# Splitting each weight unit of the second block's attention inputs with two operations of 1024 columns in place of four of 512

## The reference, cut to what matters

```
def second_block(x, g_mix, w_in, q_norm_a, ...):
    h = rms_norm(x, g_mix)
    proj = h @ w_in
    a_qkv = proj[..., :A_QKV].reshape(Bsz, S, 3, A_HEADS, HEAD_DIM_2)
    b_qkv = proj[..., A_QKV:A_QKV + B_QKV].reshape(Bsz, S, 3, B_HEADS, HEAD_DIM_2)
...
    qa = head_rms(a_qkv[:, :, 0], q_norm_a).transpose(0, 2, 1, 3)
```

## Time and profile before

| what | value |
|---|---|
| median of 3 runs | 2525.06 us |
| the profiled execution's own time | 2522.77 us |
| its span on the core | 2521.0 us |
| busy PE, DVE, ACT, POOL | 2501.6, 1684.4, 1226.2, 276.3 us |
| splits of this stage | 240 on ACT (L1491), 240 on DVE (L1863), from 1082.7 to 1450 us |

### The profile page before, as it was taken

How to read it: one execution, slowest core, us unless ns; L and a number is a source line. 1 busy time by engine, 2 the same in 40 slices (tenths; PEclk the granted TensorE clock), 3 DMA queues, 4 the chain that set the end, 5 groups by cost and what they waited for, 6 DMA issues and landing times.

```text
span 2521.0 us, 38233 instructions
## 1 busy us (share of the span) xinstructions
PE 2501.6 (99%) x13066; PEld 2134.5 (85%) x13066; DVE 1684.4 (67%) x2663; ACT 1226.2 (49%) x2144; POOL 276.3 (11%) x297
## 2 busy tenths in 40 slices
PE   9999999999999999999999999999999999999999
PEld 7888888888888888878888888888888888888888
DVE  7787889958885788576555554457575565665664
ACT  6656655434443444456566554445453443443442
POOL 0000215303330233040000000001100000000000
PEclk9999999999999999999999999999999999999999
DMA  7454545665555556646555456655465556555554
GB/s 245 159 169 162 168 134 191 194 211 183 188 193 194 186 187 192 206 125 205 183 179 177 155 175 194 196 187 198 153 216 192 192 184 200 187 197 189 187 194 134
DMA packets 197232, 463.75 MB, mean 184 GB/s; under 512 B 17482, under 2 KB 45166, under 8 KB 197102
## 3 DMA queue, kind: packets, MB, share of 16 engines
q1 hardware_dynamic: 196430, 459.91, 56.0%
q0 software_dynamic: 672, 2.11, 0.3%
HBM read 459.81 MB, written 2.14 MB: 183 GB/s over the span
## 4 chain that ended last, share of the span: by engine, by line
PE 83%; DVE 9%; issue 3%; ACT 3%; DMA 1%; DVEq 0%; SPq 0%; POOL 0%; ACTq 0%; POOLq 0%
PE G L845 46%; PE SB L845 34%; DVE wlo L1874 3%; PE MB L845 2%; DVE wlo L1863 1%; ACT y L1619 1%; ACT whi L1504 1%; DVE y L2130 1%; DMA raw<-in_in 1%; PE SB L1424 0%; DVE hS L1932 0%; DVE x L1924 0%; DMA x<-in_xT 0%; PE SB L1345 0%; DVE og L2213 0%
## 5 line engine op out<-in xcount | busy, mean ns | idle before, releaser
L1874 DVE TENSOR_TENSOR wlo<-raw,whi 128x1024 fp32r<-128x1024 f32 x446 | 546.3, 1265 | 81.6 <-ACT whi L1504 70.8
L845 PE MATMUL SB<-whi,hS 128*128 128x512 f32 x1728 | 546.8, 393 | 0.0
L845 PE MATMUL G<-hS,whi 128*128 128x512 f32 (+1 forms) x2240 | 534.5, 391 | 2.4 <-DVE hS L2331 1.2
L1871 DVE TENSOR_TENSOR wlo<-raw,whi 128x1024 fp32r<-128x1024 f32 (+1 forms) x304 | 352.1, 1199 | 262.1 <-ACT whi L1501 261.1
L1504 ACT ACTIVATE whi<-raw 128x1024 fp32r<-128x1024 f32 x446 | 449.0, 1051 | 127.9 <-PE SB L845 63.3
L845 PEld LDWEIGHTS G<-hS,whi 128*128 128x128 f32 x2240 | 409.6, 188 | 86.9 <-issue 3.4
L1501 ACT ACTIVATE whi<-raw 128x1024 fp32r<-128x1024 f32 (+1 forms) x304 | 298.7, 1029 | 352.7 <-PE SB L845 289.2
L845 PEld LDWEIGHTS SB<-whi,hS 128*128 128x128 f32 x1728 | 325.4, 188 | 67.2
L845 PE MATMUL SB<-wlo,hS 128*128 128x512 f32 x864 | 337.1, 390 | 0.0
L1605 ACT ACTIVATE tmp<-G 128x256 f32<-128x256 f32 x231 | 87.8, 380 | 503.9 <-PE G L845 503.9
L845 PE MATMUL G<-aS,whi 128*128 128x512 f32 x1248 | 300.3, 391 | 0.0
(11 more groups left out here) (237 smaller groups left out, 2281.4 us busy)
## 6 DMA issues: line engine op xcount, KB each, us to landing
raw<-in_up SPq DMA_DIRECT2D x304, 512.0 KB, 4.5
raw<-in_dn SPq DMA_DIRECT2D x216, 512.0 KB, 4.4
raw<-in_in SPq DMA_DIRECT2D x192, 256.0 KB, 3.6
raw<-in_in SPq DMA_DIRECT2D x64, 512.0 KB, 4.7
raw<-in_out SPq DMA_DIRECT2D x64, 512.0 KB, 4.4
raw<-in_mix SPq DMA_DIRECT2D x64, 512.0 KB, 4.0
raw<-in_mix SPq DMA_DIRECT2D x32, 384.0 KB, 3.7
raw<-in_in SPq DMA_DIRECT2D x32, 192.0 KB, 3.0
```

The lines of the kernel that those rows point to most:

```text
L845: return pe.matmul(o, w, m, start=start, stop=stop, skip_group_check=half_first)
L1871: dve.tensor_tensor(group_weights(wlo, slot, half, depth(st, k)), group_raw(h0 % RAW_SLOTS, depth(st, k)), group_weights(whi, slot, half, ...
L1874: dve.tensor_tensor(wlo[:, slot, a * P:b * P], raw[:, h0 % RAW_SLOTS, 0:(b - a) * P], whi[:, slot, a * P:b * P].bitcast(F32), ALU.subtract ...
```

## The change

A unit is split by two operations on ACT and two on DVE. Each covers two pieces, 1024 columns: two neighbouring slots of `raw8` are read with the row tile outside and the slot inside (8 runs of 128 columns), and 4 runs of 256 columns are written. ACT waits for both slots to have landed; each operation raises `hi_done` or `lo_done` by two. The loads, their waits and the order of everything else on every queue stay.

```diff
@@ -340,6 +340,10 @@
+        def in2_raw(at):
+
+            return raw8[:, at:at + 2, :].rearrange("p c (k n) -> p k c n", k=KPG)
+
@@ -1484,12 +1488,13 @@
                 if st.name == "in2":
                     dst = whi[:, slot, :].rearrange("p (k c n) -> p k c n", k=KPG, c=PARTS)
-                    for part in halves:
+                    for part in (0, 2):
                         j = st.piece(it, k, part) - st.pbase
-
-                        act.wait_ge(landed8[IN2_SLOT(j)], LANDED8[j])
-                        act.activation(dst[:, :, part, :], raw8[:, IN2_SLOT(j), :].rearrange("p (k n) -> p k n", k=KPG),
-                                       ACT.Copy).then_inc(hi_done, 1)
+                        at = IN2_SLOT(j)
+
+                        act.wait_ge(landed8[at], LANDED8[j])
+                        act.wait_ge(landed8[at + 1], LANDED8[j + 1])
+                        act.activation(dst[:, :, part:part + 2, :], in2_raw(at), ACT.Copy).then_inc(hi_done, 2)
                     return
@@ -1857,11 +1862,11 @@
                     h_w, l_w = (w[:, slot, :].rearrange("p (k c n) -> p k c n", k=KPG, c=PARTS) for w in (whi, wlo))
-                    for part in halves:
+                    for part in (0, 2):
                         j = st.piece(it, k, part) - st.pbase
-                        dve.wait_ge(hi_done, st.piece(it, k, part) + 1)
-                        dve.tensor_tensor(l_w[:, :, part, :], raw8[:, IN2_SLOT(j), :].rearrange("p (k n) -> p k n", k=KPG),
-                                          h_w[:, :, part, :].bitcast(F32), ALU.subtract).then_inc(lo_done, 1)
+                        dve.wait_ge(hi_done, st.piece(it, k, part) + 2)
+                        dve.tensor_tensor(l_w[:, :, part:part + 2, :], in2_raw(IN2_SLOT(j)),
+                                          h_w[:, :, part:part + 2, :].bitcast(F32), ALU.subtract).then_inc(lo_done, 2)
                     return
```

## The result

The changed kernel takes 2528.35 us (median of 20 runs, 2526.97 to 2530.97); the kernel before took 2523.43 us on the same chip (20 runs, 2522.41 to 2525.88). The ratio is 1.0019, with a 95% interval of 1.0013 to 1.0025: 4.9 us or 0.19% slower. The forecast was 2527.2 us: 4.4 us over the profiled execution of before (2522.77), and 3.8 us over this median of 20 runs.

A forecast was written before the change was run, and what follows sets the result against it. The prediction took PE, busy 2501.6 of 2521.0 us, as the bound. To the profiled execution's 2522.77 it added 1.54 us at the first turning and 2.9 for the clock: 2527.2 us, range 2522.5 to 2530.0.

The forecast's parts named there:

- Cost of an operation: Split of a unit on DVE: 2.36 us in two operations against 2.48 in four, 0.12 us gained.
- Turns of POOL and DVE: Units 4 to 6: folds and subtractions alternate strictly; a subtraction's turn takes 1.08 us for 1024 columns, 0.55 before.
- A later start: In the seam DVE waits for ACT's longer first copy; unit 4's copy starts 0.45 us later, bounds 0 and 1.2.
- Unit 4: Before group 1: two turns in place of four, PE starts 1.03 us earlier, its 2.73 us wait shrinking to 1 or 1.5.
- The row sums: After group 1's start: POOL's folds end at 1133.00, PE waits 3.34 us, and the sums come 2.36 us later.
- The clock: Behind the new wait at the row sums: 5.8 us at half clock, costing +2.9 us.
- The first turning: Attention's first turning: at 1147.32 without a wait, +1.54 us without the clock, ACT at about the old time.
- The seam's own wait: Before the second half's turning: PE's wait grows by about the later start or more, costing little at the end.
- The steady part: Units after the first turning, 350 us: three tight turnings lose 0.06 us each, 0.2 us in all.
- the clock holds: Rival: the clock stays full behind the new wait at the row sums, total 2524.4 us; chance 0.13.
- POOL is not held up: Rival at the folds: DVE lacks unit 6 or POOL gets two turns for one; 2523.1 to 2525 us, chance 0.23.
- slower: Rival: the steady part's slack is used up, turnings lose some 6 us; above 2530.1, about 2533 us; chance 0.10.

The follow-up runs named there:

- e5: Pairs on both engines in units 4 to 6 only, fours elsewhere, against the kernel before: 2525.65 us, ratio 1.0010.
- e3: Pairs on both engines in units 7 to 59 only, fours in units 0 to 6, against the kernel before: 2525.13 us, ratio 1.0007.
- e4: Pairs on both engines in units 0 to 3 only, fours elsewhere, against the kernel before: 2524.06 us, ratio 1.0001.
- e7: The changed kernel with POOL's ten folds working on one column each, run once: 2523.88 us, against 2528.25 us for the change's profiled execution.
- e8: Fours everywhere, ACT's copies of unit 4 before its eight squarings, PE's row sums four row tiles later, against the kernel before: 2521.00 us, ratio 0.9990.
- e1: ACT copies in pairs as in the change, DVE subtracts in fours as before, against the kernel before: 2526.94 us, ratio 1.0012.
- e2: DVE subtracts in pairs as in the change, ACT copies in fours as before, against the kernel before: 2528.64 us, ratio 1.0019.
- e6: The whole change with PE's row sums four row tiles later (`NORM6 = 12`, not 10), against the kernel before: 2527.55 us, ratio 1.0020.
- e9: Units 7 on divided 512, 512, 1024 on both engines, the others in fours, against the kernel before: 2524.23 us, ratio 1.0004.

## Why the prediction was right, step by step

PE's lag behind the kernel before (start of the same matmul, the lag at 1080 us taken off), at four times of the trace of before:

| kernel | 1126.5 | 1144.5 | 1158 | 1515 |
|---|---|---|---|---|
| after | -0.4 | 4.8 | 3.8 | 5.0 |
| e5 (units 4 to 6) | -1.4 | 3.9 | 2.9 | 2.9 |
| e3 (from unit 7) | 0.0 | 0.0 | 1.0 | 2.2 |
| e4 (units 0 to 3) | 0.9 | 1.0 | 1.2 | 1.2 |
| e7 (tiny folds) | -0.2 | -0.2 | -0.2 | 1.0 |
| e8 (unit 4 early, fours) | -3.8 | -3.3 | -1.7 | -1.8 |

- **Cost of an operation: right.** 2.36 us for a unit, as in the earlier trace rows; and the 120 operations less on each engine gave nothing, since PE is the bound.
- **Turns of POOL and DVE: right.** One fold, one subtraction, in strict turn, to the end of the folds. e1 (fours on DVE) and e7 (folds of one column) take the wait away, each from its side.
- **A later start: size off.** "I take 0.45 us in all for the start of unit 4's copy." It was 1121.03 - 0.48 - 1119.59 = 0.96, inside the bounds of 0 and 1.2. The two subtractions of unit 0 run back to back, and POOL's second scaling, which now starts together with them, gets no turn: 3.68 us, where it took 2.07 before and 1.58 is what it takes undisturbed. In e1 and e2, with pairs on one engine only, it takes 2.55 and 2.60 us, and PE's wait at the first half's turning is 0.2 and 0.3 us: the 1.4 us need pairs on both. PE's turning of the first half comes 1.4 us late, and DVE's addition waits for PE. So the first subtraction started 1.45 us later, not 1.04.
- **Unit 4: half right.** The wait of 2.73 us shrank to nothing, not to 1 or 1.5, because PE itself came 2.3 us late out of the seam. Where the seam was left as it was (e5) the wait was 1.3 us.
- **The row sums: place and size right.** The wait was 3.44 us (forecast 3.34). The sums were 3.2 us late, not 2.36; the rest is the later start.
- **The clock: mis-sized.** "I take the same 5.8 us at half clock behind it: +2.9." It was 3.4 us, a loss of 1.7; the wait's length, from which I took the figure, does not set that of the half clock (last section).
- **The first turning: right, for a reason that was half wrong.** PE came without a wait. But the scalings were not ready "at about the old time": they ended at 1147.85, 1.6 us later than before with the lag taken off, and only PE's own lateness covered it. To this point the balance was +3.8 us; the prediction's terms give 1.54 + 2.9 = 4.4. The later start made it more, the clock less.
- **The seam's own wait: right in effect, larger in size.** It grew from 3.4 to 4.6 + 1.4 us, yet units 0 to 3 in pairs cost only 0.6 us (e4; its interval holds zero).
- **The steady part: mis-sized.** "0.2 in all", and it was 1.2 us (e3: 1.2; e7: 1.2). I had looked at the turnings alone, and missed the output step at 1185 us, where two late splits add up.

There is luck in the total. The forecast was added to one execution (2522.77), near the median of 20 runs (2523.43); added to the median of three, 2525.06, it would have come to 2529.5. And +4.9 us against +4.4 is near because two terms that were too small (start, steady part) and one that was too large (clock) partly cancel. The mechanism and its order hold without that luck: e5 shows half of the loss with units 4 to 6 alone, e3 a third with units 7 to 59. The rival "the clock holds" was wrong by one window (0.66); "POOL is not held up" by the ten folds of 16.19 us; "slower", the used-up slack, was the right idea for the steady part at a fifth of its price.

What stays open: what decides whether half clock comes and lasts 3.4 or 6.8 us, how much of each profile's sum this is, and whether the 0.6 us of e4 are real.

## What to carry to other kernels

In this kernel merging two operations of an engine that is not the bound gained nothing. Count what gets coarser: the engine behind it starts after the whole merged operation (here a unit is done 0.35 us later, though both engines are busy for less), and an engine that takes turns with it is held off for longer (here 1.08 us in a turn in place of 0.55). When a wait is removed by moving its reader or one unit of work, look for every other reader of the same late data, on all engines, before counting the gain: of 3.7 us won by the start of group 1 in e8, 1.8 were left, and in e6 DVE's read of the sums undid the move.

## What the runs showed of the hardware

**POOL takes turns with DVE in one case and waits out a run of its operations in another.** The folds (two inputs each) alternate strictly with the subtractions. POOL's scaling (one input and a scalar) does not always. Timeline, POOL and DVE in the seam, of the kernel after and then of the kernel before:

```profile
1084.39 3.68 POOL L2530 TENSOR_SCALAR y<-y,rs 128x512 f32<-128x512 f32 x1
...
1084.36 2.36 DVE L1868 TENSOR_TENSOR wlo<-raw,whi 128x1024 fp32r<-128x1024 f32 x2 [2.27 <-ACT whi L1497]
```

```profile
1102.18 3.91 POOL L2525 TENSOR_SCALAR y<-y,rs 128x512 f32<-128x512 f32 x1
...
1102.18 2.49 DVE L1863 TENSOR_TENSOR wlo<-raw,whi 128x512 fp32r<-128x512 f32 x4
```

In the kernel after DVE starts 0.03 us ahead, runs both subtractions at full speed, and the scaling takes 3.68 us in place of 1.58: about 2.1 us of standing still, nearly all of the 2.36. The same was seen again at 1100.14 (3.63 us beside a pair of 2.36 us at 1100.05). It is not the length of DVE's operations that does it: in the kernel before, a scaling that starts together with four subtractions of 512 columns takes 3.91 us; one that starts together with two of 1024 in the kernel after (at 1103.75) takes 3.76. Where a scaling starts later than the first subtraction of its unit, as at 1083.92 and 1098.44 in the kernel before (0.6 us later), it takes 2.07 us and holds up a subtraction instead. But in e1 and e2 scalings that start within 0.2 us of the first subtraction take 2.5 to 2.6 us, so what lets POOL in stays open. The longer seam waits of the change come with where its scalings fall; longer operations alone (e2) gave 2.60 us.

**The half clock has two lengths, and the wait ahead of it does not tell which.** The granted clock fell to half (1.2 GHz) for 3.4 us or for 6.8 us at a time. The same seam waits of 4.6 and 1.4 us stood before 6.8 us in the change and in e7, and before 3.4 us in e4; the seam's 3.4 us stood before 6.8 us in the kernel before and before 3.4 us in e8. Windows of e4, and of e7:

```profile
1100.00:1105.00 5.00, 1.61 (x7) 1.44 (x8) 5.00 (x8) 3.48 (x7) 5.00 (x2) 0.86 0.56 180
1105.00:1110.00 5.00, 4.72 (x22) 3.44 (x21) 4.21 (x13) 1.57 (x5) 5.00 (x3) 0.80 0.73 239
```

```profile
1100.00:1105.00 5.00, 1.50 (x6) 1.44 (x7) 5.00 (x8) 3.58 (x7) 5.00 (x2) 0.71 0.50 160
1105.00:1110.00 5.00, 4.90 (x18) 3.55 (x17) 4.31 (x13) 1.47 (x5) 5.00 (x3) 0.61 0.76 255
```

In e4 (0.14 + 0.20) x 5 / 0.5 is 3.4 us, in e7 (0.29 + 0.39) x 5 / 0.5 is 6.8. Nor does the length of the wait say whether the clock falls: behind the 2.7 us before group 1 and the 2.4 us of e8 it stayed at 1.00, and behind e9's 1.9 us at the first turning (it ends at 1145.70) it was at 0.66. Window of e9:

```profile
1145.00:1150.00 5.00, 4.30 (x14) 3.48 (x15) 3.38 (x7) 0.47 (x1) 0.00 (x0) 0.66 0.74 230
```

The 11 single runs of e8 lie in three heaps, 2519.4 to 2519.6, 2520.4 to 2521.1 and 2522.2 to 2523.0 us, with means 1.2 and 1.9 us apart, near the 1.7 us that one stretch of 3.4 us costs; that the heaps are these stretches is argued, not shown. Whatever they are, a difference of 1 us between single profiles means little here; the medians stand in the tables.
